# Queries and keys with tokens on the partitions, normed per token and head and turned on TensorE

## The reference, cut to what matters

```python
h = rmsnorm(x, g_mix)
proj = h @ w_in                       # -> fq | fk | fv | ff | lx | lg | mq | gate_logits
q = rmsnorm(fq.reshape(b, s, 8, 128), g_q_fox)    # per token and head
k = rmsnorm(fk.reshape(b, s, 8, 128), g_k_fox)
y_fox = forgetting_attention(q, k, v, log_f)      # 8 heads, causal, bias from summed log forget gates
y_lru = rg_lru(conv(lx), ...) * gelu(lg)
mk, mv = split(rmsnorm(mem, g_mem) @ w_mem_kv, 2) # mem: 256 rows
qm = rmsnorm(mq.reshape(b, s, 4, 256), g_q_mem)   # per token and head
km = rmsnorm(mk.reshape(b, m, 4, 256), g_k_mem)
y_mem = softmax(qm @ km.T / 16) @ mv              # 4 heads
# merged by sigmoid gates, x = x + merged @ w_out, then a ConvGeGLU block of hidden width 5632
```

## Time and profile before

| | |
|---|---|
| median of 3 runs | 1657.31 us (1656.4 to 1659.15) |
| the profiled execution | 1657.26 us |
| its span in the trace | 1655.6 us |
| TensorE busy | 1639.1 us |
| VectorE busy | 1117.0 us |
| ScalarE busy | 893.2 us |
| GpSimd busy | 55.8 us |

### The profile page before, as it was taken

The page is one execution under the profiler, slowest core; times in us unless marked ns, Lnnn a source line. Parts: engine busy times, 40 slices in busy tenths (PEclk is TensorE's granted clock), DMA queues, the critical chain, the costliest instruction groups (busy, mean ns, idle before and its releaser), DMA issues.

```text
span 1655.6 us, 27015 instructions
## 1 busy us (share of the span) xinstructions
PE 1639.1 (99%) x9226; PEld 1419.2 (86%) x9226; DVE 1117.0 (67%) x1323; ACT 893.2 (54%) x1138; POOL 55.8 (3%) x57
## 2 busy tenths in 40 slices
PE   9999999999999999999999999999999999999998
PEld 7788888888888888888888888888888888888887
DVE  6976678778757466565666777777777777545443
ACT  6766667466645455445455555555555555433332
POOL 0010121000000000000001000000000000000000
PEclk9999999999999999999999999999999999999999
DMA  8545455644455555555555555555555555655553
GB/s 319 191 140 168 156 173 189 209 161 139 166 190 189 191 181 190 190 188 189 183 192 184 181 181 196 192 188 181 199 181 179 198 193 188 198 196 196 203 197 101
DMA packets 85256, 307.35 MB, mean 186 GB/s; under 512 B 9880, under 2 KB 10656, under 8 KB 85088
## 3 DMA queue, kind: packets, MB, share of 16 engines
q1 hardware_dynamic: 83952, 302.88, 55.0%
q0 software_dynamic: 1120, 3.94, 0.7%
q10 hardware_dynamic: 144, 0.01, 0.0%
HBM read 304.69 MB, written 2.11 MB: 185 GB/s over the span
## 4 chain that ended last, share of the span: by engine, by line
PE 90%; DVE 5%; DMA 2%; issue 2%; ACT 1%; SPq 0%; POOL 0%; ACTq 0%; DVEq 0%; POOLq 0%
PE psG L335 87%; PE psM L335 2%; DVE W L937 2%; DMA raw<-w_units 1%; DVE fox_rstd L967 1%; DMA xs<-xT 1%; ACT W L599 1%; DVE X L1124 0%; DMA lru_rg<-w_rg 0%; DVE x_n L1220 0%; PE psM L444 0%; ACT fox_rstd L638 0%; DVE fox_S L995 0%; DVE stat L998 0%; DVE sq L1167 0%
## 5 line engine op out<-in xcount | busy, mean ns | idle before, releaser
L335 PE MATMUL psG<-X,W 128*128 128x512 f32 (+1 forms) x5632 | 993.7, 338 | 2.9 <-DVE X L1124 2.9
L335 PEld LDWEIGHTS psG<-X,W 128*128 128x128 f32 x5632 | 860.6, 188 | 131.4 <-issue 5.7
L937 DVE TENSOR_TENSOR W<-raw,W 128x1024 fp32r<-128x1024 f32 x566 | 686.4, 1227 | 318.2 <-ACT W L599 315.5
L599 ACT ACTIVATE W<-raw 128x1024 fp32r<-128x1024 f32 x566 | 590.0, 1054 | 317.3 <-PE psG L335 309.1
L335 PE MATMUL psG<-hidden,W 128*128 128x512 f32 (+1 forms) x1408 | 245.4, 337 | 0.0
L335 PEld LDWEIGHTS psG<-hidden,W 128*128 128x128 f32 x1408 | 214.0, 188 | 31.3
L607 ACT ACTIVATE low<-psG 128x512 f32<-128x512 f32 x132 | 79.0, 598 | 216.4 <-PE psG L335 216.4
L335 PE MATMUL psG<-Y,W 128*128 x768 | 134.4, 337 | 0.0
L335 PEld LDWEIGHTS psG<-Y,W 128*128 128x128 f32 x768 | 117.0, 188 | 17.1
L1367 DVE SCALAR_TENSOR_TENSOR up_c<-up_pad,par_sb,up_c 128x256 f32<-128x256 f32 x176 | 77.5, 482 | 42.3 <-ACT up_c L881 36.3
L335 PE MATMUL psG<-merged,W 128*128 128x512 f32 (+1 forms) x512 | 89.3, 337 | 0.0
(11 more groups left out here) (190 smaller groups left out, 681.1 us busy)
## 6 DMA issues: line engine op xcount, KB each, us to landing
raw<-w_units SPq DMA_DIRECT2D x566, 512.0 KB, 3.4
xs<-xT SPq DMA_DIRECT2D x4, 512.0 KB, 8.9
outT<-xs POOLq DMA_DIRECT2D x7, 256.0 KB, 3.4
mem_raw<-first_data SPq DMA_DIRECT2D x3, 512.0 KB, 5.3
mem_raw<-memT SPq DMA_DIRECT2D x3, 512.0 KB, 8.3
lru_rg<-w_rg POOLq DMA_DIRECT2D x8, 128.0 KB, 4.2
c_all<-c_rows POOLq DMA_DIRECT2D x1, 1024.0 KB, 5.5
outT<-xs SPq DMA_DIRECT2D x2, 128.0 KB, 1.8
```

Source lines behind the costliest of these rows:

```text
L335: return nc.tensor.matmul(*a, skip_group_check=True, **kw)
L599: nc.scalar.activation(W[:, s, :, 0], raw[:, s], ACT.Copy).then_inc(hi_done, 1)
L937: V.tensor_tensor(W[:, s, :, 1], raw[:, s], f32(W[:, s, :, 0]), ALU.subtract).then_inc(lo_done, 1)
```

## The change

- Phases: mkq becomes mk and mq, qk becomes kq (four groups: keys, queries, keys, queries), all of them wide. Their results lie in psG with tokens on the partitions and 512 channels along the free axis: two memory heads or four forgetting heads.
- For each of these eight groups (j = 0 to 7; L is the group's last unit): at L+4 ScalarE squares all 1024 elements a partition from psG (`norm_squares`) and VectorE sums them per head (`norm_sums`); at L+5 ScalarE takes the root (`norm_root`) and VectorE the reciprocal and the product of psG with it (`norm`), into `normed`, which also frees psG; TensorE turns `normed` by eight transposes into psM (`turn(j)`) after the second unit of the next group; at L+6 ScalarE copies that to kT or qT times the gain (`turned_copied`).
- The sums with ones, `scale_k`, `v_cur`, GpSimd's squares and values go. The memory's inverse root mean square goes into the copy of the turned weights (`weights_copied`), its effect on eps into `mem_eps`.
- Memory attention has 2 instances of two heads in place of 4 of one. Scores come after unit 3, not 4.
- The beginning: squares of the memory at units 9 to 12, of x at 13 to 16, root of x at 24, `x_n` at 25 to 28, the parts of X at 26 to 29; the small steps for lambda move from 24 to 26 to 33 to 36.
- The loops over mkq and qk are unrolled.

```diff
-PHASES = [("mv", 1, 2, 8, 512), ("mkq", 4, 2, 4, 256), ("lru", 4, 2, 4, 256), ("v", 1, 2, 8, 512), ("qk", 4, 2, 4, 256)]
+PHASES = [("mv", 1, 2, 8, 512), ("mk", 1, 2, 8, 512), ("mq", 1, 2, 8, 512), ("lru", 4, 2, 4, 256), ("v", 1, 2, 8, 512),
+          ("kq", 1, 4, 8, 512)]
...
+NORMED = [("mk", 0), ("mk", 1), ("mq", 0), ("mq", 1), ("kq", 0), ("kq", 1), ("kq", 2), ("kq", 3)]
...
+            def turn(j, **banks_free):
+
+                def hook():
+                    if j == 0:
+                        pe.wait_ge(const_in, 48)
+                        pe.wait_ge(root_done, 1)
+                    else:
+                        pe.wait_ge(turned_out, j)
+                    side_waits(**banks_free)
+                    pe.wait_ge(evac_done, NORM_GROUP[j] + 1)
+                    for d in range(4):
+                        for t in range(2):
+                            o = d % 2 * T + t * P
+                            ins = nc.tensor.transpose(psM[:, d // 2, o:o + P], normed[:, t, d * P:(d + 1) * P], ident[:])
+                    ins.then_inc(turned, 1)
+                return hook
...
-                return {0 if kind == "fox" else 1: sums, 4: scores, 6: transposes, 7: values}
+                return {3: scores, 6: transposes, 7: values}
...
+            wide_group("mk", 0, m_op, {0: mem_sums, 4: x_sums})
+            wide_group("mk", 1, m_op, {1: turn(0)})
+            x_ready = lambda n: pe.wait_ge(xX_lo, n // 2 + 1)
+            wide_group("mq", 0, x_op, {1: turn(1)}, ready=x_ready)
+            wide_group("mq", 1, x_op, {1: turn(2), **attention_hooks("mem", 0)})
+            plain("lru", None, {1: turn(3, act=side_count("mem", 0, "act", "weights_copied")), **attention_hooks("mem", 1)})
...
+            wide_group("kq", 0, x_op, {})
+            wide_group("kq", 1, x_op, {1: turn(4, dve=side_count("decay", 0, "dve", "z"))})
+            wide_group("kq", 2, x_op, {1: turn(5), **attention_hooks("fox", 0)})
+            wide_group("kq", 3, x_op, {1: turn(6, act=side_count("fox", 0, "act", "weights_copied")), **attention_hooks("fox", 1)})
+            plain("gate0", None, {1: turn(7, act=side_count("fox", 1, "act", "weights_copied")), **attention_hooks("fox", 2)})
+            plain("gate0", 1, attention_hooks("fox", 3))
...
+            def norm_squares(kind, j):
...
+                act.wait_ge(pe_units, GROUPS[g][3] + 1)
+                nc.scalar.activation(squared[:], psG[:, 2 * (w % 2):2 * (w % 2) + 2, :], ACT.Square).then_inc(head_squares, 1)
+
+            def norm_root(kind, j):
...
+                act.wait_ge(head_summed, j + 1)
...
+                if phase == "mk":
+                    act.wait_ge(mem_eps_set, 1)
+                    for t in range(2):
+                        ins = nc.scalar.activation(head_rms[:, t, 0:2], head_ss[:, t, 0:2], ACT.Sqrt, bias=mem_eps[:, t:t + 1])
                 else:
...
+                    bias = eps[:, 1:2] if phase == "mq" else eps[:, 2:3]
+                    ins = nc.scalar.activation(head_rms[:, :, 0:heads], head_ss[:, :, 0:heads], ACT.Sqrt, bias=bias)
+                ins.then_inc(head_root, 1)
...
+            steps_at = {"normed": {3: [norm_squares], 4: [norm_root], 5: [turned_copied]}, "mem": softmax, "fox": softmax,
...
+            def norm_sums(kind, j):
+                heads = 4 if NORMED[j][0] == "kq" else 2
+                dve.wait_ge(head_squares, j + 1)
+                if j > 0:
+                    dve.wait_ge(head_root, j)
+                V.tensor_reduce(head_ss[:, :, 0:heads], square["fox" if heads == 4 else "mem"].rearrange("p t (h d) -> p t h d", h=heads),
+                                AX_X, ALU.add).then_inc(head_summed, 1)
+
+            def norm(kind, j):
...
+                dve.wait_ge(head_root, j + 1)
+                V.reciprocal(rms, rms).then_inc(head_inverse, 1)
+                dve.wait_ge(head_inverse, j + 1)
+                if j > 0:
+                    dve.wait_ge(turned, j)
+                b, d = 2 * (w % 2), 2 * UC // heads
+                V.tensor_tensor(normed.rearrange("p t (h d) -> p t h d", h=heads),
+                                psG[:, b:b + 2, :].rearrange("p t (h d) -> p t h d", h=heads),
+                                rms.rearrange("p t (h d) -> p t h d", d=1).to_broadcast([P, 2, heads, d]), ALU.mult).then_inc(evac_done, 1)
...
+            steps_at = {"normed": {3: [norm_sums], 4: [norm]}, "mem": {7: [row_max, weights], 11: [attention_lo]},
+                        "fox": {7: [row_max, weights], 11: [attention_lo]},
...
+                if u == 24:
                     dve.wait_ge(root_done, 1)
...
+                    V.reciprocal(rstd_x[:], rstd_x[:]).then_inc(rstd_done, 1)
+                if 25 <= u < 29:
+                    c = u - 25
                     dve.wait_ge(rstd_done, 1)
                     V.tensor_tensor(x_n[:, 4 * c:4 * c + 4], xs[:, 4 * c:4 * c + 4],
...
+                                    rstd_x[:].to_broadcast([P, 4, T]), ALU.mult).then_inc(x_scaled, 1)
+                if 26 <= u < 30:
+                    c = u - 26
                     dve.wait_ge(xX_hi, c + 1)
                     gained_lo(X, x_n, "g_mix", range(4 * c, 4 * c + 4)).then_inc(xX_lo, 1)
```

More of the change, by code:

```diff
@@ L65, with _attention @@
 N_PAR = _c
-def _attention(heads, pool):
-    by_head = lambda *steps: [f"{step}{h}" for h in range(heads) for step in steps]
+def _attention(masked):
+    by_head = lambda *steps: [f"{step}{h}" for h in range(2) for step in steps]
     return {
[L74 to L78, removed]
-    }
+        "pe": ["scores", "transposes", "values"],
+        "act": by_head("exp") + ["weights_copied", "y_hi"],
+        "dve": by_head(*(["masked"] if masked else []), "row_max") + by_head("row_inv", "weights") + ["y_lo"],
+        "pool": [],
+    }
+NORMED = [("mk", 0), ("mk", 1), ("mq", 0), ("mq", 1), ("kq", 0), ("kq", 1), ("kq", 2), ("kq", 3)]
+NORM_GROUP = [G0[_name] + _w for _name, _w in NORMED]
 KINDS = [
-    ("mem", 4, _attention(1, ["squares_added", "values_staged"])),
+    ("mem", 2, _attention(False)),
     ("lru", 4, {
@@ L166, in hybrid_layer_kernel, with attention_buffers @@
         mem_v = sb("mem_v", [P, 2, BW], G_0)
[L169 to L180, removed]
+        def attention_buffers(tag, bases):
+            return {n: sb(f"{tag}_{n}", shape, base) for (n, shape), base in zip(
+                [("kT", [P, BT, T]), ("qT", [P, BT, T]), ("S", [P, 2, 2, T]), ("PT", [P, 2, 2, T])], bases)}
+        att = {"mem": attention_buffers("mem", [(96 + o) * KB for o in (0, 8, 16, 20)]),
+               "fox": attention_buffers("fox", [M0 + o * KB for o in (0, 8, 16, 20)])}
         causal = lambda t: t.rearrange("p h a t -> p h (a t)")[:, :, 0:CW]
-        v_all = sb("v_all", [P, 2, BW], M0 + 22784)
+        v_all = sb("v_all", [P, 2, BW], M0 + 24 * KB)
+        normed = sb("normed", [P, 2, 2 * UC], G_0 + 12 * KB)
+        square = {"mem": sb("mem_square", [P, 2, 2 * UC], 120 * KB), "fox": sb("fox_square", [P, 2, 2 * UC], 108 * KB)}
         lx_pad = sb("lx_pad", [P, 2, 3 + T], M0)
@@ L391, in wide_group @@
                     pe.wait_ge(lo_done, u + 1)
+                    if ready is not None:
+                        ready(n)
                     wide_unit(u, n, per, 2 * (w % 2), operand)
@@ L405, in attention_hooks @@
             def attention_hooks(kind, m):
                 A = att[kind]
[L408 to L416, removed]
+                last_turn = {"mem": [2, 3], "fox": [5, 6, 7, 7]}[kind][m]
@@ L418, in scores @@
+                own_turn = {"mem": [2, 3], "fox": [5, 5, 7, 7]}[kind][m]
                 def scores():
-                    side_waits(dve=side_count(kind, m, "dve", "normed"))
+                    pe.wait_ge(turned_out, own_turn + 1)
+                    side_waits(dve=side_count(kind, m, "dve", None), act=side_count(kind, m, "act", None))
                     for qt in range(2):
                         qs = slice(qt * P, qt * P + P)
-                        if kind == "fox":
-                            keys = slice(0, qt * P + P)
-                            for h in range(2):
+                        for h in range(2):
+                            if kind == "fox":
+                                keys = slice(0, qt * P + P)
@@ L425, in scores @@
                                 dst = psM[:, 2 + h, 0:P] if qt == 0 else psM[:, 2 + h, P:CW]
[L426 to L430, removed]
+                                ins = mm(dst, A["qT"][:, 2 * m + h, qs], A["kT"][:, 2 * m + h, keys], start=True, stop=True)
+                            else:
+                                for t in range(2):
+                                    d = 2 * (2 * m + h) + t
+                                    ins = mm(psM[:, 2 + h, qt * T:(qt + 1) * T], A["qT"][:, d, qs], A["kT"][:, d],
+                                             start=t == 0, stop=t == 1)
@@ L431, in scores @@
                     done(ins)
                 def transposes():
[L434 to L437, removed]
```

(21 more changed lines are left out.)

308 lines of the change are left out of this document (132 added, 176 removed).

## The result

The changed kernel takes 1664.91 us (median of 6 runs, 1664.55 to 1665.8), the kernel before 1657.42 (6 runs beside it): ratio 1.0043, 95% interval 1.0031 to 1.0055. It is slower, by 7.5 us; the forecast was 1662.1 within 1654.5 to 1668, so it was 2.8 us too low. The profiled execution took 1664.55 us (span 1662.8), 7.3 more than the one of before.

The account below looks back on a forecast made before the run. TensorE, busy 1639.1 of 1655.6 us, was taken as the bound. 1657.26 - 14.9 (work) - 7.9 (old waits) + 8.0 (turns) + 17.9 (new waits) + 1.7 (clock) = 1662.1 us, range 1654.5 to 1668.

Parts of the forecast that it names:

- eight waits: TensorE standing at turns 0 to 7 until VectorE's multiply: 7.1, 2.95, 1.05, 1.4, 1.5, 1.05, 1.5, 1.4 us; +17.9 us.
- Units: mkq and qk: all 64 units become units of 12 products, 2.722 us in place of 2.787, -4.2 us.
- Turns: Eight turns of eight transposes on TensorE, taken at 1.0 us each (0.88 to 1.12): +8.0 us.
- Old waits: TensorE's waits for X 2.9, squares 2.4, forgetting softmax 1.7 and in mv 0.9 go: -7.9 us.
- GpSimd's queue: GpSimd still issues the gates' weights only after TensorE's last memory step, so the wait for them in lru stays.
- The clock: The granted clock falls once, behind TensorE's 7.1 us stand at turn 0: +1.7 us (0 to 3.4).
- sums: TensorE's products with ones over squares of q and k go, 10.3 us; mem_sums loses one product, 0.43 us.
- Clock holds: Rival: TensorE's stands come as worked out but the granted clock stays full: 1660.4 us; chance 0.24.
- Turns in time: Rival: six ordinary turns and turn 1 don't wait, only turn 0: 1651.3 us, or 1642.5 if none waits; chance 0.14.
- Dearer releases: Rival: each release 0.6 us dearer on eight turns, plus 1 at turn 0: 1667.9 us; chance 0.14 including the drain.
- The drain: Rival: each table load makes ScalarE's root later by one more load, 5 x 1.28 us: 1668.5 us; chance 0.04.
- Units not faster: Rival: the 0.065 us per unit belong to the v stage alone, +4.2: 1666.3 us; chance 0.06.

Follow-up runs that it names:

- the run without waits: Against the changed kernel: root and multiply one unit earlier, turn 0 and its copy three units later, turn 1 one unit later; 1641.73 us, ratio 0.9903 to before.

## Why the prediction was right, point by point

**Direction and mechanism.** Right. The kernel got slower though it does less on every engine; the forecast's eight waits are there, with the releaser that it named, and both ends of the wait were moved by experiments. Forecast 7.1, 2.95, 1.05, 1.4, 1.5, 1.05, 1.5, 1.4; measured 7.30, 2.90, 1.19, 1.60, 1.69, 1.22, 1.69, 1.62; the sum 17.9 against 19.2. The six ordinary ones were each 0.14 to 0.22 too low, turn 0 was 0.2 too low, and turn 1 0.05 too high. The chain at turn 3 shows the parts: the root takes 0.30 and not 0.25, and TensorE goes 0.14 after the end of the multiply, not 0.05.

```profile
171.48 0.31 ACT head_rms L662
...
171.81 0.19 DVE head_rms L1022
...
172.02 1.24 DVE normed L1027
173.26 0.14 issue
173.39 1.06 PE psM L430 x8
```

**Units.** Right. In the run without waits 72 products, 6 units, of the second group of kq take 16.36 us, 2.727 each, so 0.060 less than a unit of 16 products (2.787) and 3.8 us in all for 64, where the forecast had 0.065 and 4.2.

```profile
331.94 16.36 PE psG L345 x72
```

**Turns.** 1.06 us each at full clock against 1.0 taken, 0.5 for the eight.

**Old waits.** X, squares and softmax: gone, as said. In mv the text took -0.9; a wait of 0.56 us for a copy of the memory's values came (L986), because the sums of x now stand ahead of it on VectorE. The stretch up to mk is as long as before. Part of it is the first 12 us, which differ between profiled executions for no reason that the edits give: from 8 to 10 us TensorE has 10 products in the kernel before and in two of the runs above (turns one unit later, turn 0 alone later), 7 in the changed kernel, at a granted clock of 1.00 in each of them.

**GpSimd's queue.** The wait for the gates' weights was said to stay. It was 0.95 us of idle TensorE in before's profiled execution and is not there in after's, at the same order of steps; the lru and v stretch is 1.2 us shorter. The landing times of these loads spread from 2.7 to 5.4 us in after. None of the eight runs above shows it in its profile either, so that it stays is not borne out. Why it went is open, as the kernel before has only one profiled execution.

**The clock.** This is the term that was most mis-sized. The text let it fall once, behind turn 0, for 1.7 us; it fell twice, for 1.85 and 1.70. The step that failed is the one that chose where it falls: the text weighed turn 0's 7.1 us against the one stand of 2.4 us at full clock and did not weigh turn 1's 2.95, which is longer than that row too. That its price for one fall (1.7) is near what was measured is partly luck: it was taken from the first products of the kernel before, where the granted clock reads 1.00 (0 to 4.4 us), and the falls in the other runs cost 1.4 to 2.9.

By stretches, the text's terms give -0.9 up to mk, +6.9 for the memory stretch (-2.1 units, -3.9 sums, -5.3 old waits, +4.0 turns, +12.5 waits, +1.7 clock), 0 for lru and v, and -1.2 for the forgetting stretch, +4.8 in all; measured are 0.0, +9.3, -1.2 and -0.9, +7.2 in all. The memory stretch alone is 2.4 us above its terms, the clock with 1.85 and the waits with 0.5. Elsewhere the misses cancel, and that is luck: +0.9 for mv, -1.2 for lru and v (the gates' wait), +0.3 for the forgetting stretch, where the waits were 0.8 longer.

**Rivals.** Clock holds: refuted by the windows. Turns in time: refuted by the eight waits. Dearer releases: a little of it, 0.14 to 0.22 each. The drain, for which the Trainium skill (ScalarE: Activation LUTs, "What ACT_TABLE_LOAD costs") speaks: not there; an estimate by that page would have been 6.9 us more, and taking the loads away gave back 1.9 us. Units not faster: refuted (2.727).

## What to carry to other kernels

When a chain of small steps on other engines is moved behind the split that feeds the bound engine, count from what lets that split start, not from how far ahead the engines seem to be: here ScalarE could split a unit only when TensorE was done with the one four before it, which gave the release a fixed time, and turns placed ahead of that time cost 23.2 us (1664.9 against 1641.7), more than the 15.5 that the change brings. A step that only has to be ready must stand at least as many units behind its producers as its chain is long, and here it cost nothing to let all eight stand one more, since what needs their result, the scores, still stood behind them. Beginnings are the place to look twice: the same step that waited 1.2 to 1.7 us in the later groups met a queue full of other work there and waited 7.3.

## What the runs showed of the hardware

Whether the clock falls behind a stand of TensorE does not follow from the stand's length alone. In the profiled executions, without their first 15 us, it was at one half behind every stand of 3.5 us and more (3.51, 4.10, twice 4.59, 7.3 in three kernels and 7.91), and full behind every one of 1.82 and less. Between these it went either way: it fell after 2.20, 2.30 and, in four kernels, 2.9 us, and it stayed after 2.23, 2.29, before's 2.41 and one stand of 2.91. Thirteen of the fourteen falls cost 1.4 to 1.9 us, the slow turn and the slow units behind it against the same work at the full clock, and one cost 2.9. The Trainium skill (TensorE: Matmul & The Clock Gate, "HAM oscillation — how this bites in real kernels") warns of idle gaps between bursts. The runs agree that the lower level comes back behind such gaps, fourteen times here, and do not show what decides it between 2.20 and 2.91 us.
